# Four transformer layers in one kernel: first layer's projection by both token tiles per weight unit, small loads on other queues, and another order of norms and weight halves

## The reference

```python
for layer in 0, 1:                      # first block, LayerNorm behind each part
    mix = even_mixer(x, ...) if layer == 0 else odd_mixer(x, ...)
    x = layer_norm(ALPHA * x + mix, g, b)
    h = x @ ffn_w_in[layer]             # 1024 x 5632
    x = layer_norm(ALPHA * x + (silu(h[:, :2816]) * h[:, 2816:]) @ ffn_w_out[layer], g, b)
for l in 0, 1:                          # second block, RMS norms before and behind
    x = x + rmsnorm(hybrid_mixer(rmsnorm(x, pre[l]), ...), post[l])
    x = x + rmsnorm(swiglu(rmsnorm(x, ffn_pre[l]), ...), ffn_post[l])

def even_mixer(x, w_in, conv_w, pool_w, pool_scale, w_out):
    p = x @ w_in                        # 1024 x 2048
    y_a = p[:, :512] * causal_dwconv(p[:, 512:1024] * p[:, 1024:1536], conv_w)
    y_b = multiscale_pool(p[:, 1536:], pool_w, pool_scale)   # windows 2, 4, 8, 16
    return concat(y_a, y_b) @ w_out
```

## Time and profile before

| | us |
|---|---|
| median of 3 runs | 1225.51 |
| lowest, highest | 1224.81, 1229.28 |
| profiled execution, its own time | 1226.42 |
| its span | 1224.6 |
| TensorE busy | 1188.2 (97%) |
| VectorE busy | 761.3 (62%) |
| ScalarE busy | 602.3 (49%) |
| GpSimd busy | 37.9 (3%) |

### The profile page before, as it was taken

The page is one execution under the profiler, slowest core; times in us unless marked ns, Lnnn a source line. Parts: engine busy times, 40 slices in busy tenths (PEclk is TensorE's granted clock), DMA queues, the critical chain, the costliest instruction groups (busy, mean ns, idle before and its releaser), DMA issues.

```text
span 1224.6 us, 16805 instructions
## 1 busy us (share of the span) xinstructions
PE 1188.2 (97%) x5794; PEld 975.9 (80%) x5794; DVE 761.3 (62%) x1049; ACT 602.3 (49%) x916; POOL 37.9 (3%) x69
## 2 busy tenths in 40 slices
PE   6999999999999899999999999999999999999997
PEld 5777888888877788888778788888887878888886
DVE  5488555535896855463767676555455777745541
ACT  5455444425674454452465655444346465644430
POOL 0000000000000100000100110000010001000000
PEclk9999999999999999999999999999999999999999
DMA  8566755744622585564364148556626523766550
GB/s 278 176 193 208 255 172 180 240 129 138 236 92 67 174 284 176 193 231 147 123 203 156 52 148 284 188 173 218 212 82 207 167 92 120 246 202 184 168 163 34
DMA packets 163741, 214.07 MB, mean 175 GB/s; under 512 B 15857, under 2 KB 107705, under 8 KB 163680
## 3 DMA queue, kind: packets, MB, share of 16 engines
q1 hardware_dynamic: 155792, 201.44, 51.5%
q10 hardware_dynamic: 7888, 11.84, 3.0%
HBM read 212.17 MB, written 1.06 MB: 174 GB/s over the span
## 4 chain that ended last, share of the span: by engine, by line
PE 79%; DVE 10%; ACT 3%; DMA 3%; POOL 2%; issue 2%; ACTq 1%; SPq 0%; POOLq 0%; DVEq 0%
PE ps L547 24%; PE ps L549 24%; PE ps L548 24%; DVE w_lo L1393 3%; DVE o_acc L1560 2%; DMA raw<-ev_w_in 2%; PE ps L957 2%; PE ps L834 1%; POOL stat L1871 1%; ACT w_hi L1009 1%; PE ps L650 1%; POOL stat L1873 1%; PE ps L658 1%; DVE x L1432 1%; DVE x L1416 1%
## 5 line engine op out<-in xcount | busy, mean ns | idle before, releaser
L1393 DVE TENSOR_TENSOR w_lo<-raw,w_hi 128x1024 fp32r<-128x1024 f32 x380 | 449.6, 1222 | 131.3 <-ACT w_hi L1009 128.4
L1009 ACT ACTIVATE w_hi<-raw 128x1024 fp32r<-128x1024 f32 x380 | 384.3, 1054 | 138.1 <-PE ps L549 70.0
L547 PE MATMUL ps<-w_hi,a_hi 128*128 128x512 f32 x1040 | 414.5, 399 | 6.2 <-DVE w_lo L1393 2.8
L549 PE MATMUL ps<-w_hi,a_lo 128*128 128x512 f32 x1040 | 407.1, 391 | 0.0
L548 PE MATMUL ps<-w_lo,a_hi 128*128 128x512 f32 x1040 | 406.6, 391 | 0.0
L547 PEld LDWEIGHTS ps<-w_hi,a_hi 128*128 128x128 f32 x1040 | 196.1, 189 | 48.5 <-issue 3.5
L549 PEld LDWEIGHTS ps<-w_hi,a_lo 128*128 128x128 f32 x1040 | 196.0, 188 | 42.1
L548 PEld LDWEIGHTS ps<-w_lo,a_hi 128*128 128x128 f32 x1040 | 196.3, 189 | 38.6
L547 PE MATMUL ps<-w_hi,h_hi 128*128 128x512 f32 x480 | 188.7, 393 | 2.4 <-DVE h_lo L1620 1.2
L549 PE MATMUL ps<-w_hi,h_lo 128*128 128x512 f32 x480 | 187.0, 390 | 0.0
L548 PE MATMUL ps<-w_lo,h_hi 128*128 128x512 f32 x480 | 186.8, 389 | 0.0
(11 more groups left out here) (199 smaller groups left out, 727.7 us busy)
## 6 DMA issues: line engine op xcount, KB each, us to landing
raw<-ffn_w_in SPq DMA_DIRECT2D x176, 256.0 KB, 4.2
raw<-w_in SPq DMA_DIRECT2D x96, 256.0 KB, 3.2
raw<-ffn_w_out SPq DMA_DIRECT2D x88, 256.0 KB, 3.9
raw<-w_gate SPq DMA_DIRECT2D x88, 256.0 KB, 3.8
raw<-w_up SPq DMA_DIRECT2D x88, 256.0 KB, 4.5
raw<-w_down SPq DMA_DIRECT2D x88, 256.0 KB, 4.1
raw<-od_w_in SPq DMA_DIRECT2D x40, 256.0 KB, 2.9
raw<-ev_w_in SPq DMA_DIRECT2D x32, 256.0 KB, 4.9
```

The costliest lines, as they stand in the source:

```text
L547: nc.tensor.matmul(ps[:, bank, :], hi, wh, start=first, stop=False)
L549: return nc.tensor.matmul(ps[:, bank, :], lo, wh, start=False, stop=last)
L1009: nc.scalar.activation(w_hi[:, v.slot, :], raw[:, v.raw, :], ACT.Copy).then_inc(w_high, 1)
L1393: V.tensor_tensor(w_lo[:, v.slot, :], raw[:, v.raw, :], w_hi[:, v.slot, :].bitcast(F32), ALU.subtract).then_inc(w_low, 1)
```

## The change

- Layer 0, phase A: chunk 0 goes by first_rows. Each unit serves both tiles; units 0 to 2 are loaded, split and multiplied by halves of 512 columns, with own semaphores. The four halves of x are turned between them, into four banks. Chunk 1 is joint.
- Before that, TensorE does three float32 matmuls of zeros on a bank not in use (spin), around the first turn.
- SyncE loads x of tile 1 among the first units, and the seven parameter rows behind unit 3. ScalarE issues the pooling constants, pooling weights and norm rows after chunk 0 is copied, and the other constants (720 KB) in the first FFN. GpSimd issues tiny_raw (now six DMAs, one at a time), fbias and w_up, from the end of chunk 1's copies on.
- Feeds: at the boundaries one unit less before the split of x (boundary 0 on VectorE: one unit before it, in all five before the norm of tile 1, and the three units ahead of its first norm are taken away); no feed within the norm, so that at boundary 3 three units come behind it; after pooling one unit instead of three.

```diff
-            return 2 * sum(NA[:l]) + (2 * t + c if c < 2 else 2 * c + t) + 1
+            return 2 * sum(NA[:l]) + (2 * t + c if c < 2 and l > 0 else 2 * c + t) + 1
...
# SyncE
+                             l > 0 or c > 0 or q >= HALVED)
+                        if (l, c, q) == (0, 0, 0):
+                            load_x(1, 0)
+                        if (l, c, q) == (0, 0, 1):
                             load_x(0, 1)
+                            load_x(1, 1)
+                        if (l, c, q) == (0, 0, 3):
+                            for row, src in prow_rows:
+                                sp.dma_start(prow[row:row + src.shape[0], :], src).then_inc(prow_in, 16)
...
# TensorE
+            def spin(n):
+                pe.wait_ge(blank_set, 1)
+                for _ in range(n):
+                    nc.tensor.matmul(acc[:, 3, 0:SEQ], nbuf[:, 0:P], nbuf[:, P:P + SEQ], start=True, stop=True)
+            def half_unit(q, i, t):
+                pe.wait_ge(w_low if i else left_low, q + 1)
+                tok, k = slice(P * t, P * (t + 1)), 2 * q + i
+                return three_passes(IN_BANK[0][t], a_hi[:, k, tok], a_lo[:, k, tok], Unit(q), slice(CH * i, CH * (i + 1)),
+                                    k == 0, False)
+            def first_rows(hook):
+                spin(2)
+                turn_half(0, 0)
+                spin(1)
+                pe.wait_ge(x_low.sem, 1)
+                half_unit(0, 0, 0)
+                turn_half(1, 0)
+                half_unit(0, 1, 0)
+                pe.wait_ge(x_low.sem, 2)
+                half_unit(0, 0, 1)
+                half_unit(0, 1, 1).then_inc(w_used, 1)
+                half_unit(1, 0, 0)
+                half_unit(1, 0, 1)
+                turn_half(0, 1)
+                half_unit(1, 1, 0)
+                turn_half(1, 1)
+                half_unit(1, 1, 1).then_inc(w_used, 1)
...
# ScalarE
-                feed(end + (5 if is_ln[k] and not pre[k] else 6))
+                feed(end + (4 if is_ln[k] and not pre[k] else 5))
...
+                    if l == 0 and (c, t) == (0, 1):
+                        act.dma_start(const[:, C_POOL:N_CONST], a["shape_consts"][:, C_POOL:N_CONST]).then_inc(const_in, 16)
+                        act.dma_start(w_grp[:, :, :], a["ev_pool_w"][0].rearrange("g c d -> c g d")).then_inc(grp_in, 16)
+                        load_rows(0)
+                        feed(N_W - 1)
...
# VectorE
-                    feed(units)
...
-                feed(end + (5 if is_ln[k] and not pre[k] else 6))
+                feed(end + (1 if k == 0 else 4 if is_ln[k] and not pre[k] else 5))
...
                 if not (is_ln[k] and pre[k]):
-                    feed(end + 7)
-                boundary(k, 1, end + 7)
+                    feed(end + (5 if k == 0 else 7))
+                boundary(k, 1)
                 feed(end + 8)
...
-                        feed(end - 4 - (c == 2))
+                        feed(end - 4 - (3 if c == 2 else 0))
                 if LAYERS[l] == "even":
                     even_rest()
-                    feed(U_C[l] + 3)
...
# GpSimd
+            pool.wait_ge(a_out, out_at(0, 1, 1))
...
+                    if sent:
+                        pool.wait_ge(params_in, 16 * sent)
+                    nc.gpsimd.dma_start(tiny_raw[:, k, c0:c0 + w], src[:, k, :]).then_inc(params_in, 16)
```

More of the change, by code:

```diff
@@ L488, in _, with load @@
         def _(sp):
-            def load(v, left, right, split):
+            def load(v, left, right, split, whole=True):
                 if not v.first:
@@ L1014, in feed, with x_split @@
                 fed[0] = max(fed[0], min(n, U_END))
-            def x_split(kk, t, halves=(0, 1)):
-                for h in halves:
+            def x_split(kk, t):
+                for h in range(2):
                     act.wait_ge(x_turned.sem, x_turned.at(kk, 2 * t + h))
@@ L1326, in _ @@
+            half_high(1, 0)
+            half_high(1, 1)
+            first_split(0, 1)
+            half_high(2, 0)
+            first_split(1, 1)
+            half_high(2, 1)
+            fed[0] = HALVED
+            feed(8)
             for l in every:
-                order = [(0, 0), (1, 0), (0, 1), (1, 1)] + [(c, t) for c in range(2, NA[l]) for t in range(NT)]
+                order = [(0, 0), (1, 0), (0, 1), (1, 1)] if l else [(0, 0), (0, 1), (1, 0), (1, 1)]
+                order += [(c, t) for c in range(2, NA[l]) for t in range(NT)]
@@ L1398, in feed, with half_low, first_split, x_split @@
                 fed[0] = max(fed[0], min(n, U_END))
-            def x_split(kk, t, halves=(0, 1)):
-                for h in halves:
+            def half_low(u, i):
+                dve.wait_ge(w_high if i else left_high, u + 1)
+                cols = slice(CH * i, CH * (i + 1))
+                V.tensor_tensor(w_lo[:, u, cols], raw[:, u, cols], w_hi[:, u, cols].bitcast(F32),
+                                ALU.subtract).then_inc(w_low if i else left_low, 1)
+            def first_split(t, h):
+                dve.wait_ge(x_high.sem, 2 * h + t + 1)
+                part = slice(4 * h, 4 * h + 4), slice(P * t, P * (t + 1))
+                V.tensor_tensor(a_lo[:, part[0], part[1]], tb[:, 2 * h + t, :].rearrange("p (b n) -> p b n", b=4),
+                                a_hi[:, part[0], part[1]].bitcast(F32), ALU.subtract).then_inc(x_low.sem, 1)
+            def x_split(kk, t):
+                for h in range(2):
                     dve.wait_ge(x_high.sem, x_high.at(kk, 2 * t + h))
@@ L1405, in x_split, with boundary @@
                                     a_hi[:, part[0], part[1]].bitcast(F32), ALU.subtract).then_inc(x_low.sem, 1)
-            def boundary(k, t, units=0):
+            def boundary(k, t):
                 l, ffn = divmod(k, 2)
```

129 lines of the change are left out of this document (77 added, 52 removed).

## The result

The kernel after takes 1233.31 us (median of 7 runs, 1231.81 to 1236.17), the kernel before beside it 1228.87 (1224.81 to 1230.21). The ratio is 1.0047, 95% interval [1.0028, 1.0067]: 5.8 us slower, 3.4 to 8.2. The forecast was +4.3 us and called no change. Three later groups of runs, each on a chip of its own, gave the kernel before 1227.27, 1227.81 and 1226.78 us (23, 23 and 15 runs).

The account below looks back on a forecast made before the run. TensorE, busy 97% of the span, was taken to bound the kernel. Terms -6.0 - 1.7 + 3.9 + 1.8 + 4.6 + 1.7 = +4.3 us on 1225.5 gave 1229.8 us, range 1221.5 to 1233.5.

Parts of the forecast that it names:

- no change: Whole kernel: forecast 1229.8 us, within about 0.5% (6.1 us) taken as indistinguishable from no change; chance of within 0.60.
- terms 2 and 6: Clock: half of an early half-speed stretch returns, -1.7 us; one fall after the longer of two new stalls, +1.7 us.
- term 1: Start of layer 0: third chunk begins at 33.9 us instead of 39.93, -6.0 us.
- Term 2: Clock after the third chunk's start: without the 2.40 us wait, the 3.4 us half-speed stretch goes, -1.7 us.
- Their transfers about 5 us after issue: Start: weight units 4 to 7 land about 5 us after issue, ready before TensorE wants them, so both gaps go.
- term 3: Boundary 0: sixth unit's low half stands behind tile 1's norm, TensorE waits 5.4 us, x turns later, +3.9 us.
- term 4: Boundary 3: sixth unit's low half comes behind the second norm, TensorE stands still about 4.4 us, +1.8 us.
- term 5: Boundaries 2, 4, 5, 6: second norm comes later by one unit, 1.2 + 3 x 1.14, +4.6 us.
- the clock falls after both stalls: Rival: slow clock after both new stalls, or norm delays stack more; +6.0 to +8, 1231.5 to 1233.5 us; chance 0.20.
- The boundaries cost half: Rival: slack returns at the boundaries, costing about 5 instead of 10.3 us; 1223 or 1224 us; chance 0.18.
- only the start counts: Rival: order of the low halves changes nothing on the path; 1217.8 us, 1216 with warm first clock; chance 0.10.
- the late loads: Rival: GpSimd's small loads take over 4.2 us each and delay the first FFN; about 1240 us; chance 0.05.

Follow-up runs that it names:

- start: Kernel after with every feed at the boundaries and pooling as before, keeping the new start: 1221.46 us, ratio 0.9949 to before.
- restback: Kernel after with the number of units between the two norms at boundaries 1, 2, 4, 5 and 6 as before: 1228.99 us, ratio 1.0008 to before.
- k0back: Kernel after with the feeds of boundary 0 and of the pooling as before: 1227.31 us, ratio 1.0004 to before.
- k3back: Kernel after with the feeds of boundary 3 alone as before: 1232.36 us, ratio 1.0030 to before.
- busywait: Kernel after with 10 and 8 matmuls of no use where TensorE would wait at boundaries 0 and 3: 1228.88 us, ratio 1.0009 to before.
- actloads: The start kernel with GpSimd's nine small loads on ScalarE's queue again: 1219.87 us, ratio 0.9933 to before.
- keep: The start kernel with seven and four matmuls of no use before TensorE's waits at boundaries 2 and 3: 1218.99 us, ratio 0.9926 to before.
- feeds: Kernel before with the new feeds alone, without the new start: 1239.02 us, ratio 1.0091 to before.

## Why the prediction was wrong

The waits were right, place by place, and so was the sign. The forecast of +4.3 even lies inside the measured 3.4 to 8.2. Two things were wrong. The call "no change" rested on a bound of 6.1 us that no row gave; seven runs beside seven had an interval of 2.4 us to each side, and separate 5.8 from nothing. And the clock, terms 2 and 6, was to cancel (-1.7 + 1.7) but cost about 2 us net, while the boundaries cost about 1 us less than I had.

*Start (term 1, -6.0).* The trace has -5.85 at the third chunk, the runs of `start` -6.3 with the clock in it. That it fits so well is partly luck. Parts were off and made up for each other: the first weight matmul at 6.95 and not 8.05 (the four parts that I added give 7.85), and the way from there to the third chunk 27.1 us and not 25.9. Term 2 came as forecast: the clock is 1.00 from the third chunk to boundary 0.

*The late load.* "Their transfers about 5 us after issue", said of units 4 to 7, did not hold for the one at 38.66. It cost 1.99 us in the profiled execution, but 0.91, 0.65 and 0.30 in others (`restback`, `k0back`, `k3back`) and nothing that the view marks in `start`, `busywait` and `actloads`. So it is a cost that varies between 0 and 2 us, and part of why this profile is longer than the median.

*Boundary 0 (term 3, +3.9).* `k0back` gives 5.3 with its share of the clock. Seen in waits: 4.98 + 1.05 new, 1.70 + 0.44 gone, is 3.9; seen in distances at full clock, 4.0.

*Boundary 3 (term 4, +1.8).* The wait grew from 2.10 to 3.65, but at full clock the stretch is only 0.95 longer. `k3back` gives 2.1, and about half of that is the clock: from the turn of tile 0 to that of tile 1 at boundary 4 it is 141.71 us with a short slow stretch, 143.73 in the kernel after with a long one.

*Boundaries 2, 4, 5, 6 (term 5, +4.6).* 4 to 6 came to 1.14, 1.14 and 1.12, as worked out. Boundary 2 came to 1.1, nearly its 1.2: it is 13.17 us against 12.11 in `start`, both at the slow clock. Against the 11.21 of before it looks like 1.96, and the other 0.9 is the slow stretch. ("At five of seven boundaries TensorE already waits" was more than its rows show: the five waits stand at three boundaries, 0, 2 and 3.)

*The clock (terms 2 and 6, 0 in sum).* This is the step that failed. I allowed one fall behind the new waits, and priced it at 1.7, because a wait of 3.23 had left the clock alone in the one trace I had the earlier trace rows. That was one draw. The same wait, 3.18 to 3.23 us, stands in eleven profiled executions, and in all but that one half speed followed. In the kernel after three falls came in place of one, and they cost 2.1 (behind 4.98), 0.9 (behind 3.23) and 2.7 us (behind 3.65) by the table of distances, 5.7 in all, with the two long stretches twice the length that I priced. The list of runs of the kernel before shows that it falls there too: each run carries its mean granted clock, and it goes from 0.999 (1224.53 us) to 0.992 (1230.66 to 1231.62 us). Over 23 runs time and clock correlate at -0.93, and 0.6 us of time go with each microsecond of clock lost ((1 - clock) x span); two other groups of before, 23 and 15 runs, give 0.9 and 0.8. So what looked like noise of the kernel before goes for the most part with the clock (a correlation cannot say which is the cause; `busywait` and `keep` can). My base was on its quiet side: the profiled run had 0.997, the mean is 0.9954.

With that price the means can be corrected, as an estimate. After has 0.9930 against 0.9954: 2.9 us of clock lost more, worth 1.8 to 2.7 us of the 5.8, where terms 2 and 6 have 0. What is left, 3.1 to 4.0, is terms 1, 3, 4 and 5, forecast +4.3; boundary 3, at 0.95 in place of 1.8, explains part of the difference. `busywait` agrees from the other side: at a clock of 0.997, 4.9 us less of it lost than after, it is 4.7 us faster. The same correction on `k0back` (0.9948, worth 1.4 to 2.0) leaves 3.3 to 3.9 for term 3. The 1.5 us between 4.3 and 5.8 are less than the interval of the measurement, so it is the traces and not the medians that show this step.

The Trainium skill ("TensorE: Matmul & The Clock Gate", HAM oscillation) says that waits for data between bursts bring the slow clock back for the next burst. The prediction weighed that rule against the one row at 3.23 and went by the row. The traces agree with the rule: both long stalls pay, as it said, with 2.1 and 2.7 us in place of 1.7 each.

Of the rivals, "the clock falls after both stalls" (0.20; 1231.5 to 1233.5) comes nearest: +6 to +8 against 5.8, and it names the cause. "The boundaries cost half" (5 us) and "only the start counts" are refuted by the 11.2 us of `feeds`, the late loads by GpSimd's rows.

## What to carry to other kernels

Before a change is forecast to within half a per cent, look at the spread of the kernel's own runs against the clock of each: one profile shows one draw of it. In a kernel like this one, price a wait of TensorE of 2 us or more as its length plus a slow stretch behind it, which cost 0.9 to 2.7 us here, at most half of its length. Where the wait cannot be removed, matmuls of no use in it win that back (here 2.8 us for 11 and 4.7 us for 18 of them). And when work is moved behind a long serial step on one engine, ask which consumer needs the *next* piece: here one unit's low half moved behind a norm stalled TensorE for 5 us, while the five before it were early. And look at the timeline of each experiment for what its edit really moved: `restback` left out the boundary that it was also meant for, and only the unchanged wait of 3.64 us told.

## What was not expected of the hardware

- The same wait of 3.18 to 3.23 us was followed by full clock in one execution and by half speed (1.2 GHz; 0.72 over 6 us in after) in ten. Behind waits of 2.08 to 2.10 us the clock fell in four executions of five, behind 1.57 to 1.95 us ahead of the turn of tile 0 at boundary 0 in one of seven, behind 3.60 to 4.98 us in all ten cases. The slow stretches are 3.4 or 6.8 us long.
- The run-to-run spread of the kernel before, 1224 to 1233 us, follows the mean granted clock (correlations -0.93, -0.92, -0.90).
- A weight load of 256 KB took 7.8 us in the median with broadcast rows beside it, and its lateness changed from run to run: ScalarE waited 4.25 us for one unit in one execution, and 3.33, 1.88, 0.84 or not at all in others.
- Small loads issued by GpSimd, each waiting for the last, followed each other in 2.6 to 6.2 us; no row of before had shown one.
